# Stick-breaking attention: suffix sums from fp32r products of high and low parts, one step later

## The reference, cut to what matters

```
z = (q . k) * scale ;  mask: k < q
log_rem = where(mask, log_sigmoid(-z), 0)
suffix  = reverse_cumsum_over_k(log_rem) - log_rem
a       = where(mask, exp(log_sigmoid(z) + suffix), 0)
out     = a @ v
```

## Time and profile before

| | us |
|---|---|
| median of 3 runs | 1957.16 (1956.93 to 1964.48) |
| the profiled execution | 1958.32 |
| its span, first to last instruction | 1956.4 |
| PE busy | 1915.2 (98%) |
| PEld busy | 1638.5 (84%) |
| DVE busy | 771.0 (39%) |
| ACT busy | 706.9 (36%) |
| POOL busy | 712.7 (36%) |
| mean granted clock of TensorE | 0.995 |

### The profile page before, as it was taken

One profiled execution on the slowest core, in us unless ns is written; L12 is line 12 of the kernel. 1 busy time (PEld: TensorE's weight loads), 2 busy tenths in 40 slices (PEclk: granted clock), 3 DMA queues, 4 the chain that ended last, 5 costly groups with the idle time before them and its releaser, 6 DMA issues.

```text
span 1956.4 us, 26806 instructions
## 1 busy us (share of the span) xinstructions
PE 1915.2 (98%) x11012; PEld 1638.5 (84%) x11012; DVE 771.0 (39%) x1309; ACT 706.9 (36%) x1328; POOL 712.7 (36%) x343
## 2 busy tenths in 40 slices
PE   9999989999998999999999999999999999999999
PEld 9999878989987897888888878889867878888887
DVE  6433473454326536531102254645676441111010
ACT  4112455321225545323222322535565552222221
POOL 5333210353331014555554432420003345555443
PEclk9999899999999999999999999999999999999999
DMA  4222100122221002222222333210003212222223
GB/s 155 87 77 87 55 1 1 65 78 86 79 85 44 1 12 92 97 93 91 97 95 89 97 104 126 82 44 1 1 1 108 87 65 97 90 93 97 92 93 107
DMA packets 40586, 144.23 MB, mean 74 GB/s; under 512 B 4624, under 2 KB 4880, under 8 KB 40336
## 3 DMA queue, kind: packets, MB, share of 16 engines
q1 hardware_dynamic: 40464, 142.51, 21.9%
HBM read 140.40 MB, written 2.10 MB: 73 GB/s over the span
## 4 chain that ended last, share of the span: by engine, by line
PE 90%; DVE 5%; ACT 3%; issue 1%; DMA 1%; POOL 0%; SPq 0%; DVEq 0%; ACTq 0%
PE ps L354 23%; PE ps L355 23%; PE ps L356 23%; PE ps L897 5%; PE ps L878 5%; PE ps L887 3%; PE ps L2078 1%; PE ps L2050 1%; PE ps L2061 1%; PE ps L1822 1%; PE ps L519 1%; PE ps L1015 1%; DVE scratch L497 1%; ACT scratch L915 0%; DVE nm L936 0%
## 5 line engine op out<-in xcount | busy, mean ns | idle before, releaser
L350 POOL TENSOR_TENSOR wl<-raw,wh 128x1024 fp32r<-128x1024 f32 (+2 forms) x254 | 604.0, 2378 | 814.1 <-ACT wh L342 814.1
L354 PE MATMUL ps<-xh,wh 128*128 128x512 f32 (+2 forms) x1720 | 615.0, 358 | 3.1 <-POOL wl L350 2.2
L342 ACT ACTIVATE wh<-raw 128x1024 fp32r<-128x1024 f32 (+2 forms) x254 | 266.1, 1048 | 956.6 <-PE ps L356 892.2
L355 PE MATMUL ps<-xl,wh 128*128 128x512 f32 (+2 forms) x1720 | 609.4, 354 | 0.0
L356 PE MATMUL ps<-xh,wl 128*128 128x512 f32 (+2 forms) x1720 | 607.8, 353 | 0.0
L354 PEld LDWEIGHTS ps<-xh,wh 128*128 128x128 f32 x1720 | 323.6, 188 | 57.1 <-issue 5.9
L355 PEld LDWEIGHTS ps<-xl,wh 128*128 128x128 f32 x1720 | 323.8, 188 | 49.0 <-issue 1.8
L356 PEld LDWEIGHTS ps<-xh,wl 128*128 128x128 f32 x1720 | 324.1, 188 | 47.3
L1142 POOL TENSOR_TENSOR xl<-xb,xh 128x512 fp32r<-128x512 f32 (+1 forms) x22 | 26.1, 1187 | 332.8 <-ACT xh L1051 332.8
L355 PE MATMUL ps<-aL,wh 128*128 128x512 f32 x352 | 139.4, 396 | 0.0
L356 PE MATMUL ps<-aH,wl 128*128 128x512 f32 x352 | 139.2, 396 | 0.0
(11 more groups left out here) (355 smaller groups left out, 2662.2 us busy)
## 6 DMA issues: line engine op xcount, KB each, us to landing
raw<-wstream SPq DMA_DIRECT2D x236, 512.0 KB, 3.4
raw<-wstream SPq DMA_DIRECT2D x16, 384.0 KB, 3.0
raw<-wstream SPq DMA_DIRECT2D x10, 528.0 KB, 3.4
h<-xT SPq DMA_DIRECT2D x4, 528.0 KB, 6.4
out<-h SPq DMA_DIRECT2D x8, 256.0 KB, 4.0
hm<-memT SPq DMA_DIRECT2D x1, 1024.0 KB, 4.8
cst<-const SPq DMA_DIRECT2D x1, 720.5 KB, 9.5
cst<-const SPq DMA_DIRECT2D x1, 320.0 KB, 3.8
```

The costliest lines, as they stand in the source:

```text
L342: e.activation(wh[p % 2][:, 0:n], raw[c % 2][:, 0:n], ACT.Copy).then_inc(*w_hi(p))
L350: e.tensor_tensor(wl[p % 2][:, 0:n], raw[c % 2][:, 0:n], wh[p % 2][:, 0:n].bitcast(F32), ALU.subtract).then_inc(*w_lo(p))
L354: e.matmul(o, w_h, x_h, start=start, stop=False)
L355: e.matmul(o, w_h, x_l, start=False, stop=False)
```

## The change

Softplus no longer goes to the products in fp32. It is split into a high part SPh, rounded to fp32r, and a low part SPl, the difference, and both are multiplied in fp32r with the triangular matrix and with the matrix of -1, of which fp32r copies triR and negR are made once (their entries 0 and -1 are exact). The running total RT is gone: for block j TensorE adds the product of -1 with the high and the low part of each later block i = 3 to j + 1, so a block has 2 (4 - j) products instead of two. ScalarE makes the high part for j = 3 and 2, right behind the Exp and Ln of the next step; VectorE makes it for j = 1 and 0, right behind its own softplus add; GpSimd makes every low part. The softplus sum is written into Ab, and SPb shrinks to two alternating buffers. The sums and the probability are three steps behind the scores instead of two and the value products four instead of three, with the scores begun one step ahead instead of two, so that TensorE's program keeps its order of blocks. GpSimd makes an output's low part after the low part of block 3 of the second head behind it (heads 3, 5, 7), the last output's at the end.

```diff
--- before.py
+++ after.py
@@ -256,9 +256,11 @@
         Pb2 = sb("Pb2", [128, 4, L], at=nsa)
         PT2 = [sb(f"PT2{i}", [128, 640], at=nsa) for i in range(2)]
         nsa.close()
-        SPb = sb("SPb", [128, 2, 4, T], at=two)
+        SPb = sb("SPb", [128, 2, T], at=two)
         Ab = sb("Ab", [128, 2, 4, T], at=two)
-        RT = sb("RT", [128, 2, T], at=two)
+        SPh = sb("SPh", [128, 2, 4, T], F32R, at=two)
+        SPl = sb("SPl", [128, 2, 4, T], F32R, at=two)
+        triR, negR = (sb(n, [128, 128], F32R, at=two)[:, :] for n in ("triR", "negR"))
         two.close()
         mid.close()
         mem = ExitStack()
@@ -2041,6 +2043,15 @@
             k = SB.index((a, j))
             return PS[:, 512 * sb_bank(k):512 * sb_bank(k) + T - 128 * j]
 
+        def sb_high(a, j):
+
+            return (x_hi if j > 1 else v_out)["sb", "high", a, j]
+
+        def sb_low_free(on, a, j):
+
+            if a >= 2:
+                on.wait_ge(*one_mm["suffix", a - 2, 0])
+
         def sb_pe(e, on):
             def begin(k):
                 a, j = SB[k]
@@ -2051,23 +2062,24 @@
                 on.wait_ge(*a_one["strict"])
                 e.matmul(ps[:, 0:128], identR[:, :], strictR, start=False, stop=True).then_inc(*score("sb", a, j))
             begin(0)
-            begin(1)
-            for k in range(len(SB) + 3):
-                if 2 <= k < len(SB) + 2:
-                    a, j = SB[k - 2]
+            for k in range(len(SB) + 4):
+                if 3 <= k < len(SB) + 3:
+                    a, j = SB[k - 3]
                     u, q0 = a % 2, 128 * j
                     n, ps = T - q0, sb_psum(a, j)
-                    on.wait_ge(*v_out["sb", "sp", a, j])
-                    r = e.matmul(ps, C("tri"), SPb[:, u, j, 0:n], start=False, stop=True, skip_group_check=True)
-                    if j < 3:
-                        on.wait_ge(*v_out["sb", "rt", a, j + 1])
-                        r = e.matmul(ps[:, 128:n], C("negone"), RT[:, u, q0 + 128:T], start=False, stop=True,
+                    on.wait_ge(*a_one["tri"])
+                    for i in range(3, j, -1):
+                        for part in (SPh, SPl):
+                            e.matmul(ps[:, 128 * (i - j):n], negR, part[:, u, i, 0:T - 128 * i], start=False, stop=True,
                                      skip_group_check=True)
+                    for part, done in ((SPh, sb_high(a, j)), (SPl, x_lo["sb", "sp", a, j])):
+                        on.wait_ge(*done)
+                        r = e.matmul(ps, triR, part[:, u, j, 0:n], start=False, stop=True, skip_group_check=True)
                     r.then_inc(*one_mm("suffix", a, j))
-                if k + 2 < len(SB):
-                    begin(k + 2)
-                if k >= 3 and SB[k - 3][1] == 0:
-                    a = SB[k - 3][0]
+                if k + 1 < len(SB):
+                    begin(k + 1)
+                if k >= 4 and SB[k - 4][1] == 0:
+                    a = SB[k - 4][0]
                     u, t_ = a % 2, a // 2
                     if u == 0:
                         claim(on, 6 + t_ % 2, 1, a_out["sb", "out", t_])
@@ -2080,7 +2092,9 @@
                     r.then_inc(*pv("sb", a))
 
         def sb_act(e, on):
-            for k in range(len(SB) + 3):
+            e.activation(triR, C("tri"), ACT.Copy)
+            e.activation(negR, C("negone"), ACT.Copy).then_inc(*a_one("tri"))
+            for k in range(len(SB) + 4):
                 if k < len(SB):
                     a, j = SB[k]
                     e_ = Ab[:, a % 2, j, 0:T - 128 * j]
@@ -2088,12 +2102,18 @@
                     e.activation(e_, e_, ACT.Exp).then_inc(*a_out("sb", "exp", a, j))
                     on.wait_ge(*a_out["sb", "exp", a, j])
                     e.activation(e_, e_, ACT.Ln, bias=1.0).then_inc(*a_out("sb", "ln", a, j))
-                if 2 <= k < len(SB) + 2:
-                    a, j = SB[k - 2]
+                if 1 <= k < len(SB) + 1 and SB[k - 1][1] > 1:
+                    a, j = SB[k - 1]
+                    on.wait_ge(*v_out["sb", "sp", a, j])
+                    sb_low_free(on, a, j)
+                    e.activation(SPh[:, a % 2, j, 0:T - 128 * j], Ab[:, a % 2, j, 0:T - 128 * j], ACT.Copy).then_inc(
+                        *x_hi("sb", "high", a, j))
+                if 3 <= k < len(SB) + 3:
+                    a, j = SB[k - 3]
                     on.wait_ge(*one_mm["suffix", a, j])
                     e.activation(Ab[:, a % 2, j, 0:T - 128 * j], sb_psum(a, j), ACT.Exp).then_inc(*prob("sb", a, j))
-                if k >= 3 and SB[k - 3][1] == 0 and SB[k - 3][0] % 2:
-                    a = SB[k - 3][0]
+                if k >= 4 and SB[k - 4][1] == 0 and SB[k - 4][0] % 2:
+                    a = SB[k - 4][0]
                     t_ = a // 2
                     f, before = place(("sb", t_))
                     on.wait_ge(*pv["sb", a])
@@ -2108,13 +2128,13 @@
                 if k < len(SB):
                     a, j = SB[k]
                     u, n = a % 2, T - 128 * j
-                    o, sp = sb_psum(a, j), SPb[:, u, j, 0:n]
+                    o, sp = sb_psum(a, j), SPb[:, k % 2, 0:n]
                     on.wait_ge(*score["sb", a, j])
                     if k == 0:
                         on.wait_ge(*turn["nsa1", 3])
                         on.wait_ge(*v_end["nsa1", 3, "gate"])
-                    if a >= 2:
-                        on.wait_ge(*one_mm["suffix", a - 2, 0])
+                    if k >= 2:
+                        on.wait_ge(*v_out[("sb", "sp") + SB[k - 2]])
                     e.tensor_scalar(sp, o, 0.0, None, ALU.max, ALU.bypass).then_inc(*v_out("sb", "max", a, j))
                     on.wait_ge(*v_out.now())
                     if a >= 2:
@@ -2124,32 +2144,29 @@
                 if 1 <= k < len(SB) + 1:
                     a, j = SB[k - 1]
                     u, n = a % 2, T - 128 * j
-                    sp = SPb[:, u, j, 0:n]
+                    t = Ab[:, u, j, 0:n]
                     on.wait_ge(*a_out["sb", "ln", a, j])
-                    e.tensor_tensor(sp, sp, Ab[:, u, j, 0:n], ALU.add).then_inc(*v_out("sb", "sp", a, j))
-                if 2 <= k < len(SB) + 2:
-                    a, j = SB[k - 2]
-                    u, q0 = a % 2, 128 * j
-                    n = T - q0
-                    sp = SPb[:, u, j, 0:n]
-                    on.wait_ge(*v_out["sb", "sp", a, j])
-                    if j == 3:
-                        if a >= 2:
-                            on.wait_ge(*one_mm["suffix", a - 2, 0])
-                        e.tensor_copy(RT[:, u, 384:512], sp).then_inc(*v_out("sb", "rt", a, 3))
-                    elif j:
-                        on.wait_ge(*one_mm["suffix", a, j])
-                        on.wait_ge(*v_out["sb", "rt", a, j + 1])
-                        e.tensor_copy(RT[:, u, q0:q0 + 128], sp[:, 0:128])
-                        e.tensor_tensor(RT[:, u, q0 + 128:T], RT[:, u, q0 + 128:T], sp[:, 128:n], ALU.add).then_inc(
-                            *v_out("sb", "rt", a, j))
+                    e.tensor_tensor(t, SPb[:, (k - 1) % 2, 0:n], t, ALU.add).then_inc(*v_out("sb", "sp", a, j))
+                    if j <= 1:
+                        on.wait_ge(*v_out.now())
+                        sb_low_free(on, a, j)
+                        e.tensor_copy(SPh[:, u, j, 0:n], t).then_inc(*v_out("sb", "high", a, j))
 
         def sb_pool(e, on):
-            for t_ in range(4):
+            def outputs(t_):
                 f, _ = place(("sb", t_))
                 on.wait_ge(*x_hi["ao", "sb", t_])
                 e.tensor_tensor(xl[:, 4 + t_, M:L], fin[:, f, 0:T], xh[:, 4 + t_, M:L].bitcast(F32),
                                 ALU.subtract).then_inc(*x_lo("ao", "sb", t_))
+            for k, (a, j) in enumerate(SB):
+                u, n = a % 2, T - 128 * j
+                sb_low_free(on, a, j)
+                on.wait_ge(*sb_high(a, j))
+                e.tensor_tensor(SPl[:, u, j, 0:n], Ab[:, u, j, 0:n], SPh[:, u, j, 0:n].bitcast(F32),
+                                ALU.subtract).then_inc(*x_lo("sb", "sp", a, j))
+                if j == 3 and a in (3, 5, 7):
+                    outputs(a // 2 - 1)
+            outputs(3)
 
 
         def mix_ao(k):
```

## The result

The changed kernel takes 1961.97 us, the median of 22 runs (1960.18 to 1965.01). The kernel before, run beside it, takes 1957.72 (22 runs). The ratio is 1.0019, with a 95% interval of 1.0012 to 1.0026: the change costs 2.3 to 5.1 us. That is real, but it lies inside the 0.5% that the prediction called "same". The forecast was 1959.

The account below looks back on a forecast made before the run. TensorE was taken as the bound, its shed 0.85 us per head turning into waits for probabilities. Net +1.6 us for the stage and 0.3 for the ramp, +1.9 on the median of 1957.16, gave 1959 us; range 1951 to 1966.

Parts of the forecast that it names:

- rival B: Stick-breaking stage: VectorE slower, copies at 0.69 us and blocked adds paying their whole duration behind GpSimd; 1962 us, chance 0.17.
- TensorE's own time: TensorE's work per head in the stage, forecast to fall from 8.22 to 7.37 us with the fp32r products.
- The blocking: VectorE's softplus adds with two SBUF inputs stand still while GpSimd subtracts, ending 0.15 to 0.55 us behind it.
- ScalarE's order as the second link: ScalarE's queue: the probability of j = 0, 0.64 us, comes only behind newer Exp 0.55, Ln 0.43 and high part 0.32.
- The two loops: Latest-ending paths between heads' value products: 8.27 us, or 8.61 with an output's low part; two heads 16.88 against 16.93.
- the value products at the loop's start: TensorE's eight value products of a head, a term of 2.26 us in each loop.
- the short loop: Path between value products through the blocked add of j = 3 and ScalarE's queue: 8.27 us.
- the long loop: Path between value products where GpSimd also makes an output's low part, through the blocked add of j = 2: 8.61 us.
- The ramp: Stage opening: first max of j = 0 to first value products 8.98 us, 1.96 late; 0.3 added for the clock.
- A: Rival: blocking absent or looser in the stage, 7.80 us per head; 1954.5 us, chance 0.27.
- C: Rival: idle gaps halve TensorE's clock; 2009 us throughout, or 1963.5 in ramp and first head alone; chance 0.05.
- D: Rival: the stage's fp32r products run at fp32's speed, TensorE 11.8 us per head; 1984 us, chance 0.01.

Follow-up runs that it names:

- e4: Changed kernel with the softplus add taking one input from PSUM and ScalarE making the probability ahead of the newer Exp and Ln: 1952.07 us.
- e1: Changed kernel, but the softplus add takes max(z, 0) afresh from PSUM, leaving one SBUF input; TensorE's sums wait for it: 1956.06 us.
- e2: Changed kernel, but GpSimd fills the softplus low parts with zeros in place of subtracting: 1956.88 us.
- e8: Kernel before the change, with GpSimd also doing the changed kernel's 32 subtractions into an unread tile and outputs' low parts at the changed kernel's places: 1959.61 us.
- e6: Changed kernel with sums and probabilities two steps behind the scores again, value products three, and two scores made ahead: 1964.11 us.
- e3: Changed kernel, but ScalarE makes the probability of three steps back ahead of the newer step's Exp, Ln and high part: 1960.09 us.
- e7: Changed kernel with the add from PSUM, the probability first and the outputs' low parts one subtraction sooner on GpSimd: 1951.80 us.

## Why the prediction was right

**The number.** 1961.97 lies at the upper edge of the forecast's 1957 to 1962, where rival B had its 1962 too. The time alone doesn't tell them apart; the profile does. The forecast was 1.9 us over the kernel before, and the measurement is 4.2 over it. The stage, 72 us in the bounds of the earlier trace rows, took 75.6, just under the 76 at which the prediction would have failed.

**What bounds.** Right. TensorE lost 5.1 us of busy time in the stage, and none of it reached the end.

**TensorE's own time.** 7.37 us per head was forecast and 7.52 measured (e4). The new products take 2.87 for 2.76: 0.17, 0.51 and 0.86 with -1, and 0.29, 0.35, 0.46 and 0.23 triangular. The value of 0.12 for 256 columns was a little low.

**The blocking.** Shown in three ways: one operand from PSUM takes it away (e1), so does taking GpSimd's subtraction away (e2), and giving GpSimd idle work brings it into the kernel before (e8). In the changed kernel it makes the adds 24.1 us instead of 15.5. The Trainium skill says as much ("SBUF — State Buffer", Who interferes with whom): an operation of VectorE with two SBUF inputs contends with a GpSimd instruction that reads SBUF, one with at most one SBUF input outside the two-port modes doesn't, and a copy can when it runs in a two-port mode. Here e1 agrees with the second (284 ns for 760) and e8 with the third (390 for 225).

**ScalarE's order as the second link.** Shown by e1 and e4: with plain adds the heads are still 8.1 us apart, and with the probability first as well 7.52.

**The two loops.** They are the ones that ended latest, in the order in which the prediction has them, but 8.58 and 8.98 us instead of 8.27 and 8.61. From the first to the last value products this made 58.6 for 56.6, and that is the whole miss of the stage, which was forecast 1.6 us longer and is 3.6 longer. The mis-sized term is the value products at the loop's start. The prediction took 2.26, from the 2.21 of the earlier trace rows. But the chain's pieces inside one engine run from the end of one record to the end of the next, not from start to start, as the part on the profile before has it. In e4 the piece is 1421.76 to 1423.97, while the record of the eight is 1421.59 to 1423.96, and 0.16 us of it overlap the product before. So 2.21 leaves out what the product before hides, and it holds only where TensorE goes on without a stop. In the changed loop TensorE stands still ahead of the eight, and nothing hides their start: the chain above has 2.44, and the argument starts at 1422.03, 2.53 after their start. That is +0.27 in each loop. It isn't a matter of what follows them: in e6's chain ScalarE waits for the end of the eight, and with scores right ahead of them the piece is 2.22. The earlier trace rows had the longer number too, in the last value products (2.42), ahead of which TensorE had waited for ScalarE. (The ends of these records are modelled; the start of the argument is measured.) The Trainium skill has the mechanism ("TensorE: Matmul & The Clock Gate", Single matmul latency): a single bf16 product takes a constant of some 166 ns beyond its columns at full clock. By it, as an estimate, the term would have been 2.21 + 0.17, near 2.4; the traces, with 2.44 for these fp32 products, agree. In the short loop the other differences nearly cancel: the wait behind GpSimd until the next max is 0.26 for 0.18, the argument 0.29 for 0.23, Ln to high part 0.52 for 0.43, the probability 0.53 for 0.64, the add and the copy 1.14 for 1.22. In the long loop the high part of 256 columns takes 0.42 for 0.32 as well, again an operation ahead of which its engine stood still.

**The ramp.** 14.24 us forecast (5.26 + 8.98), with 0.3 on top for the clock; 14.20 measured. That it fits is luck, since two errors cancel in it: the first max of j = 0 came 4.80 us after the first score (before: 5.26), and from it to the value products it took 9.40 for 8.98.

**The rivals.** A (no blocking) is not this kernel, but it is e1: forecast 1954.5 for such a loop at 7.80, measured 1956.06 at 8.1. B's slow copies are absent (426 ns). C, the clock, is absent past the ramp in this kernel's profile, and it is closer than its 0.05 says: at the end of e3 the granted clock fell to half after TensorE had been busy 2.11 and then 1.79 us of two stretches of 3 us, with no gap over 0.85 us, while the changed kernel has a gap of 1.55 us there and kept 1.00. D is excluded by e4, whose fp32r products take 2.87 us per head.

**What stays open.** That the blocked adds, and not some other effect of the subtractions, are the link in the changed kernel is shown by e1. Which of GpSimd's accesses, reads or writes, does the blocking isn't. Nor is it on record how many runs of e3 and e6 lost time to the clock as their profiles did.

## What to carry to other kernels

Before work is given to an idle GpSimd, list what VectorE runs beside it: an operation with two SBUF inputs, or a copy within SBUF, stood still here for as long as a subtraction lasted that had begun before it, and taking one input of the add from PSUM freed it. When the bounding engine is relieved, walk the whole loop over all engines and ask in each queue whether what the bound waits for stands behind newer work; relieving one of two late links shortened the stage by 5.7 or 3.7 us here, both by 9.8. When a term of a walk comes from a chain of waits, see whether the engine stood still ahead of the piece: behind other work on its engine the same products made a piece of 2.21 us, from a standstill 2.44. And when a median and a stage disagree, look at the granted clock behind the stage.

## What the runs showed of the hardware that was not expected

- The blocking goes both ways. In e8 GpSimd's subtraction of 512 columns took 1467 ns on average for the 1276 of the earlier trace rows; six of the eight took 1.52 us, each begun 0.02 to 0.03 us after an add of VectorE with two SBUF inputs, which kept its 0.41 to 0.42 us. In e2 an output's subtraction took 1.54 in the same way.
- A copy of 128 columns within SBUF, 0.225 us by itself, took up to 1.18 beside a subtraction (e8), although it has a single input.
- The granted clock can fall at the end of the stage, with no long standstill: to half in e3 and e6, which cost e3's profile 3.0 us.
- The clock of the ramp differs between profiles of nearly the same work. In the stretch below e4 was granted 1.00 and e7 0.50; in the 3 us before it TensorE had been busy 0.76 us in e4 and 1.16 in e7. The two kernels don't differ in the ramp, and their first value products came after 11.73 and 12.46 us, so some 0.7 us of a comparison of two single profiles here is the clock's. The first row is e4, the second e7.

```profile
1402.00:1405.00 3.00, 3.00 (x16) 2.05 (x15) 2.16 (x6) 1.70 (x6) 1.02 (x1) 1.00 0.00 0
```

```profile
1402.00:1405.00 3.00, 3.00 (x10) 2.21 (x10) 2.28 (x6) 2.03 (x7) 1.28 (x1) 0.50 0.01 3
```
